# Two chained layers in fp32: the pool mixer's memory keys and queries made with tokens on the partitions, and a memory preparation moved

## What is computed

```python
def memory_attention(xq, mem_k, mem_v):
    ...
    s = jnp.einsum('bshd,bmhd->bhsm', q, mem_k).astype(jnp.float32) * (X_HEAD_DIM ** -0.5)
    p = jax.nn.softmax(s, axis=-1)
    o = jnp.einsum('bhsm,bmhd->bshd', p.astype(mem_v.dtype), mem_v)

def pool_layer(h, w_in, w_group, scale, w_out, mem_k, mem_v):
    proj = h @ w_in
    u, xq = proj[..., :D_MODEL], proj[..., D_MODEL:]
    mix = multiscale_pool(u, w_group, scale)
    xo = memory_attention(xq, mem_k, mem_v)
    return jnp.concatenate([mix, xo], axis=-1) @ w_out

# in first_block, for each layer i, with mem_n = rmsnorm(mem, mem_norm_g)
    kv = mem_n @ mem_w_kv[i]
    mem_k = kv[..., :X_WIDTH]   # 4 heads of 128
    mem_v = kv[..., X_WIDTH:]
...
# in second_block
    x = x + rms_norm(mix, g_post_mix[l])
    mem_n = rms_norm(mem, g_mem[l])
    c = cross_attention(h, mem_n, w_cq[l], w_ckv[l], w_co[l])
```

## Time and profile before

| | us |
|---|---|
| runs of the kernel | 1418.56, 1419.28, 1419.42 |
| median | 1419.28 |
| the profiled execution | 1418.27 |
| its span in the trace | 1416.5 |
| PE busy | 1403.6 (99%) |
| VectorE busy | 857.3 (61%) |
| ScalarE busy | 704.9 (50%) |
| POOL busy | 259.8 (18%) |

### The profile page before, as it was taken

One profiled execution on the slowest core, in us unless ns is written; L12 is line 12 of the kernel. 1 busy time (PEld: TensorE's weight loads), 2 busy tenths in 40 slices (PEclk: granted clock), 3 DMA queues, 4 the chain that ended last, 5 costly groups with the idle time before them and its releaser, 6 DMA issues.

```text
span 1416.5 us, 18653 instructions
## 1 busy us (share of the span) xinstructions
PE 1403.6 (99%) x7200; PEld 1190.3 (84%) x7200; DVE 857.3 (61%) x1035; ACT 704.9 (50%) x981; POOL 259.8 (18%) x504
## 2 busy tenths in 40 slices
PE   9999999999999999999999999999999999999998
PEld 7888889988888888888889888888887989888886
DVE  5656565756555565555656565555796655565554
ACT  6554454445444454444555555444555554644443
POOL 1022210002222222222012113222201100132222
PEclk9999999999999999999999999999999999999999
DMA  9765654455655656665544446665553553366562
GB/s 349 290 213 201 219 186 156 166 185 192 221 201 198 218 196 215 207 220 198 180 149 150 139 168 258 216 222 200 186 177 136 188 179 134 125 228 225 197 220 74
DMA packets 71655, 275.55 MB, mean 195 GB/s; under 512 B 17392, under 2 KB 37232, under 8 KB 40848
## 3 DMA queue, kind: packets, MB, share of 16 engines
q1 hardware_dynamic: 57168, 259.57, 51.6%
q0 software_dynamic: 14400, 14.81, 3.4%
HBM read 259.88 MB, written 1.05 MB: 184 GB/s over the span
## 4 chain that ended last, share of the span: by engine, by line
PE 95%; ACT 2%; DVE 1%; issue 1%; DMA 0%; POOL 0%; SPq 0%; DVEq 0%; POOLq 0%; ACTq 0%
PE prod L1140 16%; PE prod L1141 16%; PE prod L1144 15%; PE acc L1144 10%; PE acc L1140 10%; PE acc L1141 10%; PE prod L1134 5%; PE prod L1136 5%; PE prod L1135 5%; PE acc L1338 1%; PE acc L1159 1%; ACT w_hi L1493 1%; PE acc L1358 1%; DVE w_lo L1743 0%; PE o_bank L1394 0%
## 5 line engine op out<-in xcount | busy, mean ns | idle before, releaser
L1743 DVE TENSOR_TENSOR w_lo<-raw,w_hi 128x2048 fp32r<-128x2048 f32 x233 | 533.6, 2291 | 383.4 <-ACT w_hi L1493 380.8
L1493 ACT CAST w_hi<-raw 128x2048 fp32r<-128x2048 f32 x233 | 444.2, 1907 | 431.6 <-PE prod L1144 182.1
L1140 PE MATMUL prod<-w_hi,acts_h 128*128 128x512 f32 x944 | 370.2, 392 | 2.5 <-DVE w_lo L1752 1.8
L1144 PE MATMUL prod<-w_hi,acts_l 128*128 128x512 f32 x944 | 367.7, 389 | 0.0
L1141 PE MATMUL prod<-w_lo,acts_h 128*128 128x512 f32 x944 | 367.4, 389 | 0.0
L1004 POOL DMA_DIRECT2D four<-four x408 | 200.1, 498 | 602.4 <-DVE four L1904 585.3
L1140 PE MATMUL acc<-w_hi,mix_h 128*128 128x512 f32 x600 | 236.0, 393 | 0.0
L1144 PE MATMUL acc<-w_hi,mix_l 128*128 128x512 f32 x600 | 233.7, 390 | 0.0
L1141 PE MATMUL acc<-w_lo,mix_h 128*128 128x512 f32 x600 | 233.5, 389 | 0.0
L1140 PEld LDWEIGHTS prod<-w_hi,acts_h 128*128 128x128 f32 x944 | 177.2, 188 | 43.0 <-issue 6.9
L1144 PEld LDWEIGHTS prod<-w_hi,acts_l 128*128 128x128 f32 x944 | 177.2, 188 | 37.5 <-DVE acts_l L1814 0.3
(11 more groups left out here) (277 smaller groups left out, 1261.7 us busy)
## 6 DMA issues: line engine op xcount, KB each, us to landing
raw<-in_weights_dram SPq DMA_DIRECT2D x234, 1024.0 KB, 5.0
four<-four SPq DMA_DIRECT2D x408, 16.0 KB, 2.1
four<-four POOLq DMA_DIRECT2D x408, 16.0 KB, 1.9
raw<-in_weights_dram SPq DMA_DIRECT2D x16, 256.0 KB, 6.9
work<-in_mem_dram POOLq DMA_DIRECT2D x2, 1024.0 KB, 13.5
grow<-in_gain_rows_dram POOLq DMA_DIRECT2D x4, 512.0 KB, 3.7
tabs<-in_tabs_dram POOLq DMA_DIRECT2D x1, 1632.0 KB, 9.9
work<-in_x_t_dram SPq DMA_DIRECT2D x4, 256.0 KB, 5.7
```

The source lines that it names most:

```text
L1140: pe.matmul(out, still_hi, wh, start=first, stop=False, skip_group_check=True)
L1144: return pe.matmul(out, still_lo, wh, start=False, stop=last, skip_group_check=True)
L1493: act.copy(w_hi[:, c % RING], raw[:, c % RAW]).then_inc(hi_done, 1)
L1743: dve.tensor_tensor(w_lo[:, c % RING], raw[:, c % RAW], w_hi[:, c % RING].bitcast(F32), ALU.subtract).then_inc(lo_done, 1)
```

## The change

Three pairs of column chunks become pairs of token chunks: the memory keys of both layers and the queries of the pool mixer. `project_turned` plans them. ScalarE copies the product to a buffer in an order of blocks (`obuf[:, 0:4]`), VectorE transposes all its 32x32 blocks into `sq[:, 0:4]`, and 16 transfers (eight on SP behind a weight load, eight on POOL) carry them to the partitions of their features. The queries' norm and factor come as a column that POOL makes (`scales`). The queries' pair is now before the memory values. The keys and pool queries then lie with their tokens eight elements (32 bytes) apart, and the score matmuls read them so (`keys_of`, `tokens_of`). Waits are added for the moves: PE before the scores, ScalarE before copying out a later token projection and in later `prep`s, VectorE before it reuses the buffer. Apart from this, the first half of the second memory's preparation goes from before `scale_x` to behind the first chunk of `w_out_2`.

```diff
+
+    def project_turned(self, source, col, dest, at, buffers, of="x", mid=None, between=None, scales=None):
+
+        for k_half in range(2):
+            self.chunk("rows_half", (*source, "half", (k_half, col)), mid, e=self.e, k_half=k_half, dest=dest, at=at,
+                       of=of, acts=self.acts if of == "x" else self.mem, free=self.bank_free(2), turned=self.turned,
+                       buffers=buffers, scales=scales)
+            self.used(of)
+            if between and k_half == 0:
+                between()
+        self.turn_behind[self.c + RAW] = self.items[-1]
+        self.turned += 1
+        for t in range(2):
+            self.bank_reader.append(("cut_done", 2 * self.turned - 1 + t))
+        self.e += 2
+
+    def scales(self, factors):
+        at = self.n_scales
+        self.n_scales += len(factors)
+        self.add("scales", factors=factors, at=at, stat=self.stat)
+        return list(range(at, at + len(factors)))
 
...
-    kv_keys(0)
+    pl.project_turned(("mem_w_kv", 0), 0, "mem_k", 0, "pool", of="mem")
+    w = ("pool_w_in", 0)
+    pl.project_turned(w, D, "xq", 0, "pool", scales=pl.scales([P ** -0.5]))
     kv_values(0)
     pl.spread("x")
-    w = ("pool_w_in", 0)
-    for n in range(2):
-        pl.project(w, D + n * COLS, "xq", 2 * n, factors=(P ** -0.5,) * 2)
-    units = mem_units(4, P, "xq")
+    units = mem_units(4, P, "xq", q_blocks=True, k_blocks=True)
...
-    pl.project(("mem_w_kv", 1), 0, "mem_k", 4, of="mem")
-    pool()
-    pl.project(("mem_w_kv", 1), COLS, "mem_k", 6, of="mem")
+    pl.project_turned(("mem_w_kv", 1), 0, "mem_k", 4, "pool", of="mem", between=pool)
     pool()
     kv_values(1, between=lambda: pool_split((6, 7, 4, 5)))
...
-    memory = mem_units(4, P, "xq", 1)
+    memory = mem_units(4, P, "xq", 1, k_blocks=True)
...
-    pl.mem_prep("g_mem", [4, 5, 6, 7], [8, 9, 10, 11], "mem2")
     pl.add("scale_x", stat=pl.stat)
     pl.project_tokens(w, 2560, "rg", 0, mid=slot, between=lambda: end(slot))
...
     downs(slot, "w_out_2", 0, order,
-          lambda n: n == 1 and pl.mem_prep("g_mem", [0, 1, 2, 3], [4, 5, 6, 7], "mem2"))
+          lambda n: n < 2 and pl.mem_prep("g_mem", *(([4, 5, 6, 7], [8, 9, 10, 11]), ([0, 1, 2, 3], [4, 5, 6, 7]))[n],
+                                          "mem2"))
...
+        def cut_tokens(it, t):
+            return cut_buffer(it, 0).rearrange("p (b t k j) -> p t k b j", b=4, t=2, k=4)[:, t]
+
+        def in_cut_order(ap):
+            return ap.rearrange("p (k b j) -> p k b j", k=4, b=4)
+
+        def in_tokens(name, tile):
+
+            four_tiles = dests[name][:, tile // 4 * 4:tile // 4 * 4 + 4].rearrange("p a b -> p (a b)")
+            return four_tiles.rearrange("p (i t k) -> p k t i", t=2, k=4)[:, tile % 4]
+
+        def keys_of(name, blocks, rows, tile, width):
+            if not blocks:
+                return dests[name][rows, tile, 0:width]
+            if width == P:
+                return in_tokens(name, tile)[rows, 0]
+            return in_tokens(name, tile)[rows]
+
...
+        def move_features(engine, it, token_blocks, done):
+
+            to = dests[it["dest"]][:, it["at"]:it["at"] + 4].rearrange("p a b -> p (a b)")
+            engine.wait_ge(features_turned, it["turned"] + 1)
+            for a in token_blocks:
+                for b in range(4):
+                    engine.dma_start(to[32 * b:32 * b + 32, a * S:(a + 1) * S],
+                                     cut_buffer(it, 1)[32 * a:32 * a + 32, b * S:(b + 1) * S]
+                                     ).then_inc(done, 16)
...
                 if c < N:
                     sp.wait_ge(lo_done, c - RAW + 1)
                     sp.dma_start(raw[:, c % RAW], weights[c]).then_inc(raw_loaded[c % RAW], 16)
+                if c in plan.turn_behind:
+                    move_features(sp, plan.turn_behind[c], (0, 1), early_features_moved)
...
+                elif kind == "rows_half" and it["k_half"] and it.get("turned") is not None:
+                    move_features(pool, it, (2, 3), late_features_moved)
+                elif kind == "scales":
+                    pool.wait_ge(rstd_done, it["stat"])
+                    for n, factor in enumerate(it["factors"]):
+                        ins = pool.tensor_scalar(scales[:, 2 * (it["at"] + n):2 * (it["at"] + n) + 2], rstd["x"], factor,
+                                                 None, ALU.mult)
+                    ins.then_inc(scales_done, len(it["factors"]))
...
+                    if unit["moved"]:
+                        pe.wait_ge(early_features_moved, 128 * unit["moved"])
+                        pe.wait_ge(late_features_moved, 128 * unit["moved"])
...
-                                mm = pe.matmul(bank[:, at:at + width], dests[q][r0:r1, qt + n, t * P:(t + 1) * P],
-                                               dests[k][r0:r1, kt + n, 0:width], start=(n == 0),
-                                               stop=(n == unit["tiles"] - 1))
+                                mm = pe.matmul(bank[:, at:at + width],
+                                               tokens_of(q, unit["q_blocks"], slice(r0, r1), qt + n, t),
+                                               keys_of(k, unit["k_blocks"], slice(r0, r1), kt + n, width),
+                                               start=(n == 0), stop=(n == unit["tiles"] - 1))
...
+                    elif kind == "rows_half" and it["k_half"] and it.get("turned") is not None:
+                        if it["scales"]:
+                            act.wait_ge(scales_done, it["scales"][-1] + 1)
+                            columns_of = [scales[:, 2 * n:2 * n + 2] for n in it["scales"]]
+                        else:
+                            act.wait_ge(rstd_done, it["stat"])
+                            columns_of = [rstd["x" if it["of"] == "x" else "mem"]]
+                        if it["turned"]:
+                            act.wait_ge(features_turned, it["turned"])
+                        for t in range(2):
+                            if t:
+                                act.wait_ge(chunk_used, it["c"] + 1)
+                            else:
+                                act.wait_ge(half_done, it["half"])
+                            to, source = cut_tokens(it, t), in_cut_order(prod_flat[(it["e"] + t) % 2])
+                            if len(columns_of) == 1:
+                                ins = act.activation(to, source, ACT.Copy, scale=columns_of[0][:, t:t + 1])
...
                     elif kind == "rows_half" and it["k_half"]:
+                        if it["moved"]:
+                            act.wait_ge(early_features_moved, 128 * it["moved"])
+                            act.wait_ge(late_features_moved, 128 * it["moved"])
...
                 elif kind == "prep":
                     flush(state["target"] - 1)
+                    if it["moved"] and it["resid"] != "post":
+                        act.wait_ge(early_features_moved, 128 * it["moved"])
+                        act.wait_ge(late_features_moved, 128 * it["moved"])
...
+                    elif kind == "rows_half" and it["k_half"] and it.get("turned") is not None:
+                        dve.wait_ge(cut_done, 2 * it["turned"] + 2)
+                        if it["turned"]:
+                            dve.wait_ge(early_features_moved, 128 * it["turned"])
+                            dve.wait_ge(late_features_moved, 128 * it["turned"])
+                        dve.transpose(cut_buffer(it, 1).rearrange("p (b i n) -> p b n i", b=4, n=8),
+                                      cut_buffer(it, 0).rearrange("p (b n j) -> p b n j", b=4, n=8)
+                                      ).then_inc(features_turned, 1)
```

39 lines of the change are left out of this document (29 added, 10 removed).

## The result

The changed kernel took 1425.23 us (median; 1424.77 to 1426.34), the kernel before 1419.28 us: a ratio of 1.0045, 95% interval 1.0030 to 1.0059. It is slower by 0.45%. The forecast was 1417.9 us with a range of 1415.6 to 1421.0, so the time lies outside it, on the other side. The profiled executions differ by 1425.23 - 1418.27 = 6.96 us, their spans by 1423.4 - 1416.5 = 6.9 us.

A forecast was written before the change was run, and what follows sets the result against it. TensorE, busy 99% at full clock, was taken as the bound; -1.9 (chunks) + 0 (moves) + 0 (stride) - 1.1 (old stall) + 1.6 (new stall) = -1.4 us, from 1419.28 to 1417.9 us, range 1415.6 to 1421.0.

The forecast's parts named there:

- Part 1: Memory keys of both layers and pool queries: six column chunks become token chunks, 1.9 us less on PE.
- Part 2: Pool mixer: copies, block transposes and transfers replacing the evacuation stay hidden, costing 0; by its bounds 0 to 1 us.
- second rival: Pool mixer: moves not hidden, up to 1 us at each of two places, +2, 1419.9 us; chance 0.14.
- Part 3: Score matmuls of pool and differential mixers: operands 32 bytes apart cost 0, bounded by 0 and +6.9 us.
- third rival: The 32 score instructions: strided keys slow them, +6.9 us if the pace doubles, 1424.8 us; chance 0.12.
- Part 4: Third mixer's last projection: moving the memory preparation removes a 1.08 us PE stall and makes one of 1.6 to 1.7.
- new stall: PE's head transposes in the down projection wait for the fourth head's scaling behind the moved preparation: 1.6 to 1.7 us.
- Old stall: PE's wait for the VectorE subtraction that frees a bank, with preparation ahead of it, goes away: -1.08 us.
- first rival: Down projection: the fourth head's scaling is not held up, no stall returns, sum -3.0, 1416.3 us; chance 0.14.

The follow-up runs named there:

- e1: The changed kernel with memory scores of both mixers reading neighbouring elements again (output differs), all else as changed: 1417.26 us, ratio 0.9989 to the kernel before.
- e7: The changed kernel with each of a move's 16 transfers cut into two of half the bytes: 1436.57 us, ratio 1.0128 to the kernel before.
- e3: The kernel before with only the first half's memory preparation moved behind the first down chunk: 1418.86 us, ratio 1.0003 to the kernel before.
- e4: The changed kernel with block transposes writing runs of 32 elements, moved into natural order so scores read contiguously: 1417.39 us, ratio 0.9990 to the kernel before.
- e5: The kernel of e4 with both memory preparation halves one down chunk later: 1415.67 us, ratio 0.9981 to the kernel before.

## Why the prediction was wrong, step by step

**Part 1, the matmuls: right.** -1.9 us predicted for six chunks, -2.06 measured (before against e1, pool mixer).

**Part 2, the moves: cost right, its terms too small.** Timelines of SP, ScalarE and PE of the changed kernel, where the second pair ended at 214.09:

```profile
217.19 5.83 SPq L1030 DMA_DIRECT2D obuf<-sq  x8
...
224.29 0.69 ACT L1660 ACTIVATE mem_v<-prod,stats 128x512 f32<-128x512 f32 x1 [2.58 <-DMA obuf<-sq]
...
225.34 0.36 PE L1207 MATMUL prod<-acts_h,w_hi 128*128 128x256 f32 x1
```

The transpose took 2.18 us where I took 1.4, SP's eight issues 5.83 where I took 4.7, and the first value copy started at E+10.2 instead of E+9.0. PE starts the matmul that needs the bank 0.36 us after that copy ends; I had said 1.5 us. I also set only 0.7 us of VectorE time against each transpose as saved; the two multiplies that go took 0.69 us each, so a transpose costs VectorE 0.8 us net, and it stayed hidden. The second rival (moves not hidden) was that close, but it did not happen. e7 shows what is behind the cover: 8.5 us of waits and a lower clock.

**Part 3, the stride: this step failed.** I bounded it by 0 and +6.9 us and took 0, "because these reads are already at about half the streaming rate, so that a slower fetch has room to hide". That was an argument, not a row. A slow contiguous pace says nothing of spare room: these matmuls take 0.215 us contiguous, 0.455 with strided keys and 0.48 with strided queries too, 2.1 to 2.2 times. The term is +8.3 us, more than my upper end, and score rows over 0.3 us apart are what I had named as a sign of being wrong. The third rival had the mechanism, the place and nearly the time (1424.8; it came out at 1425.2). That it came so near is partly luck: its 6.9 us for the stride was 1.4 too small, and the medians came out 1.0 us closer together (5.95) than the profiled executions (6.96). I gave it 0.12 although the rule of the Trainium skill that I weighed there (Advanced Engine Details and Errata, section SBUF Cachelines) names this very pattern and no row spoke against it. The range left its outcome out for that reason. A stated rule against an unmeasured hope deserved something like half the chance.

**Part 4, the preparation: right, its new stall 0.2 us too large.** Old stall -1.08; new stall predicted 1.6 to 1.7. ScalarE, VectorE and PE of the changed kernel at that place:

```profile
1109.87 1.70 ACT L1773 ACTIVATE mix_h<-obuf,vecs 128x256 fp32r<-128x256 f32 x4
...
1110.41 1.68 DVE L2107 SCALAR_TENSOR_TENSOR mix_l<-obuf,vecs,mix_h 128x256 fp32r<-128x256 f32 x4 [3.21 <-ACT mix_h L1773]
1112.01 2.28 DVE L1848 TENSOR_TENSOR w_lo<-raw,w_hi 128x2048 fp32r<-128x2048 f32 x1
1114.21 0.60 DVE L2190 SCALAR_TENSOR_TENSOR sq<-prod,head_stats,work 128x128 f32<-128x128 f32 x2
...
1113.23 0.39 PE L1217 MATMUL acc<-w_hi,mix_l 128*128 128x512 f32 x1
1114.87 0.55 PE L1549 MATMUL aux<-tabs,sq 128*128 128x128 f32 x3 [1.25 <-DVE sq L2190]
```

The chain is link for link the one of the prediction (compare): scalings on ScalarE, four subtractions and a split on VectorE, then the head scaling. PE lost 1114.87 - 1113.23 - 0.23 = 1.41 us. Net +0.33, in e3 +0.32. The changed kernel has +0.53 in this stage. The rest is one wait put down to issue, ahead of an attention head's scores (L1414, operands of 64x128): 0.40 us, against 0.19 before and 0.18 in e3. It is 0.39 in e1 and e4 too, which read no stride, and e3 has the preparation moved, so neither of the two makes it. The kernels with 0.4 or more also have two more semaphore waits on PE ahead of every head's scores (`unit["moved"]`, long satisfied here); that these take the 0.2 us is likely, but no run leaves them out. The first rival (the stall absent) did not happen; e5 shows what it is worth, 1.5 us.

**The sum.** -2.06 (matmuls) + 0 (moves) + 0.53 (third mixer) + 0.22 (a later first mark, which varies by itself) = -1.31 us, and the stride's +8.27: +6.96, the difference of the two profiled executions. Everything but one term of the sum stood, within 0.2 us each, and that term was six times the rest.

## What to carry to other kernels

Before an fp32 matmul operand is read with a stride, look at how many of its elements lie within 16 bytes. Where each element of the moving operand has 16 bytes of its own, count twice the time for that matmul (other types were not run), or order the data so that runs stay whole, which here cost PE nothing even through the transfers. A term for which the profile has no row, and for which only a rule or only a hope speaks, is the one to put the chance and the range on. A wait list that hardly changes while the time grows by 7 us says to look at the pace of busy rows, and marks common to both kernels find the stage to 0.1 us.

## What the runs showed of the hardware that I had not expected

- An fp32 matmul of 256 moving columns went from 0.215 us to about 0.455 when its moving elements were 16 or 32 bytes apart, and hardly changed at 8 bytes; the change is one step. The one such matmul that lay wholly at 1.2 GHz (e7) took 0.47 us, against 0.46 at 2.4 GHz.
- A run of 128 bytes is as good as a contiguous row for the moving operand (127.50 and 127.49 us in the pool mixer). The stationary operand 32 bytes apart cost 0.19 us for four matmuls in one mixer and 0.07 in another; the difference lay in the first of the four, whose load began 0.12 us ahead in the one and 0.23 in the other.
- A VectorE block transpose of 128x1024 that writes 32 bytes apart took 2.18 us, and 1.25 us when it writes runs of 32 elements.
- A wait of 5.2 us of PE cost 2.3 us more through the lower granted clock behind it (0.50 from 232 to 238 us in e7); behind the waits of 1.5 and 1.8 us in the same run it was 1.00.
